# A hybrid encoder step on one core: the MLP's up projection in seven half-size products, its weight sums made by DMAs, and the last stage laid out anew

## What is computed

```python
p = einsum('btd,de->bte', rmsnorm(x, norm_mix), w_in)      # 10 column groups
...                                                        # heads A (stick-breaking), B (chunk band), C (HGRN2)
h = x + einsum('bte,ed->btd', mixed, w_o)                  # w_o: 1024 x 1024
u = relu(einsum('btd,df->btf', rmsnorm(h, norm_ffn), w_up))  # w_up: 1024 x 4096
y = h + einsum('btf,fd->btd', u * u, w_down)               # w_down: 4096 x 1024
```

## Time and profile before

| | us |
|---|---|
| executions | 3015.17, 3015.88, 3016.10 |
| median | 3015.88 |
| span of the profiled execution | 3009.8 |
| TensorE busy / VectorE busy / ScalarE busy / GpSimd busy | 2917.5 / 1630.4 / 987.6 / 327.6 |
| last stage, from its first transpose to the end | 1688.2 |

### The profile page before, as it was taken

One profiled execution on the slowest core, in us unless ns is written; L12 is line 12 of the kernel. 1 busy time (PEld: TensorE's weight loads), 2 busy tenths in 40 slices (PEclk: granted clock), 3 DMA queues, 4 the chain that ended last, 5 costly groups with the idle time before them and its releaser, 6 DMA issues.

```text
span 3009.8 us, 45644 instructions
## 1 busy us (share of the span) xinstructions
PE 2917.5 (97%) x18136; PEld 2585.7 (86%) x18136; DVE 1630.4 (54%) x2259; ACT 987.6 (33%) x1826; POOL 327.6 (11%) x504
## 2 busy tenths in 40 slices
PE   7999899899999999879999999999999999999999
PEld 5788788788888999768999999889999997888887
DVE  5554354476566577844444544544445445455555
ACT  3331266455555333233222222222222222232221
POOL 2322200020001255620000000000000000000000
PEclk9999999999999999989999999999999999999999
DMA  7833332453223553513211211332111213333332
GB/s 257 257 130 123 107 90 71 126 159 112 73 86 91 174 153 111 184 68 112 70 57 57 82 59 71 133 104 72 56 57 59 82 70 110 118 126 126 126 133 98
DMA packets 285061, 327.29 MB, mean 109 GB/s; under 512 B 53644, under 2 KB 234478, under 8 KB 284850
## 3 DMA queue, kind: packets, MB, share of 16 engines
q1 hardware_dynamic: 284850, 324.38, 32.8%
HBM read 256.28 MB, written 67.78 MB: 108 GB/s over the span
## 4 chain that ended last, share of the span: by engine, by line
PE 54%; DVE 1%; ACT 0%; issue 0%; POOL 0%; POOLq 0%; ACTq 0%
PE mf_psO L2260 28%; PE mf_psT L2312 23%; PE mf_psO L2312 1%; PE mf_psO L2283 1%; PE mf_psT L2246 1%; PE mf_psO L2295 0%; ACT mf_whi L2040 0%; DVE mf_wlo L2119 0%; DVE mf_acc L2212 0%; DVE mf_acc L2222 0%; DVE mf_xlo L2131 0%; ACT mf_hs L2101 0%; DVE mf_acc L2141 0%; DVE mf_hs L2149 0%; ACT mf_xhi L2055 0%
## 5 line engine op out<-in xcount | busy, mean ns | idle before, releaser
L2212 DVE TENSOR_TENSOR mf_acc<-mf_psO,mf_acc 128x1024 f32<-128x1024 f32 x256 | 313.5, 1225 | 347.8 <-PE mf_psO L2260 346.7
L2312 PE MATMUL mf_psT<-mf_xhi,mf_wlo 128*128 128x384 f32 (+1 forms) x1440 | 459.7, 319 | 0.0
L2312 PE MATMUL mf_psT<-mf_xlo,mf_whi 128*128 128x384 f32 (+1 forms) x1440 | 459.6, 319 | 0.0
L2312 PE MATMUL mf_psT<-mf_xhi,mf_whi 128*128 128x384 f32 (+1 forms) x1440 | 459.4, 319 | 0.0
L2260 PE MATMUL mf_psO<-mf_whi,mf_uhi 128*128 128x512 f32 x1024 | 401.5, 392 | 4.0 <-DVE mf_acc L2212 2.2
L2260 PE MATMUL mf_psO<-mf_whi,mf_ulo 128*128 128x512 f32 x1024 | 399.3, 390 | 0.0
L2260 PE MATMUL mf_psO<-mf_wlo,mf_uhi 128*128 128x512 f32 x1024 | 399.2, 390 | 0.0
L2040 ACT ACTIVATE mf_whi<-mf_st 128x2048 fp32r<-128x2048 f32 x104 | 194.8, 1911 | 605.1 <-PE mf_psO L2260 603.2
L2312 PEld LDWEIGHTS mf_psT<-mf_xhi,mf_whi 128*128 128x128 f32 x1440 | 270.5, 188 | 1.6
L2312 PEld LDWEIGHTS mf_psT<-mf_xlo,mf_whi 128*128 128x128 f32 x1440 | 270.5, 188 | 1.6
L2312 PEld LDWEIGHTS mf_psT<-mf_xhi,mf_wlo 128*128 128x128 f32 x1440 | 270.5, 188 | 0.0
(11 more groups left out here) (209 smaller groups left out, 5536.8 us busy)
## 6 DMA issues: line engine op xcount, KB each, us to landing
mf_st<-in_w_up SPq DMA_DIRECT2D x48, 1024.0 KB, 6.4
mf_st<-in_w_down SPq DMA_DIRECT2D x48, 1024.0 KB, 4.9
wst<-in_w_in SPq DMA_DIRECT2D x24, 1024.0 KB, 5.3
pj_wst<-in_w_in SPq DMA_DIRECT2D x36, 512.0 KB, 6.1
scratch_proj<-pj_ob SPq DMA_DIRECT2D x48, 256.0 KB, 2.0
pj_xin<-in_x_prompt SPq DMA_DIRECT2D x16, 512.0 KB, 7.3
md_qn<-scratch_proj SPq DMA_DIRECT2D x64, 128.0 KB, 2.6
scratch_proj<-md_ob SPq DMA_DIRECT2D x64, 128.0 KB, 3.3
```

Of the source, the lines that this page charges most:

```text
L2212: nc.vector.tensor_tensor(acc[0:r, i, :], psO[k % 2][0:r, :], acc[0:r, i, :], ALU.add).then_inc(s["o_out"], 1)
L2312: last = nc.tensor.matmul(up_psum(t, f, b, cn), wa[b4][:, w0:w0 + P], xa[:, j, c0:c0 + cn], start=j == 0 and q == 0, stop=j == KD - 1 and ...
```

## The change

**The up projection.** w_up is taken as two by two blocks of 512 rows and 2048 columns (W11, W12 above, W21, W22 below), and a third's frames as even tiles and odd tiles. The product of two by two blocks is made of seven products of half-size blocks in place of eight, by a variant of Strassen's form. Step p now has the features p and p + 16. Its seven products are 1 (W11), 2 (W21), 4 (W22), 5 (W12 + W22), 6 (W11 + W12 + W22), 7 (W11 + W12) and 3 (the sum of all four), each 12 matmuls of 384 (272) columns (`up`, 4 blocks of 128 rows and three parts). The frames' side has seven factors too: four are the blocks, and three (`full_sum`, `hi_sum`, `lo_sum`; with `xh6` four slots per pair of tiles) are sums, made per pair of tiles as the output projection goes on.

**PSUM.** Products 6, 5 and 3 are added on top of product 1 in one bank. Before each of them ScalarE copies what stands there (`snap`), and TensorE waits for it. VectorE adds up the four results (`add`, four instructions), ScalarE does relu and the high part of the square, VectorE squares and subtracts (`lo_u`).

**The sums of w_up** are made in HBM (`scratch_sums`, 4 x 4 MB): GpSimd issues four copies at turn 8 of `plan`, two adding DMAs at a third of it, one at its half, one at two thirds. It waits for the copies ahead of the first addition, and for each addition ahead of the next.

**The last stage.** Weights of the up projection come in chunks of 256 KB (512 rows of 512 bytes) to four staging places, and are split in 512 columns into seven pairs `uw`; those of the down projection are split in four parts. The weights of w_o lie over `u` and `uw`, so two of their four pieces can be split only after all down projections of the third before. x is loaded to `acc`. Each tile's second transpose stands in the middle of the next tile's output projection. The last third begins with the new frames, and their w_down is read from the same staging place as the other tiles'.

```diff
+            def begin_sums():
+                for out, half in copied:
+                    nc.gpsimd.dma_start(out, half).then_inc(sum_begun, 16)
+
+            def add_halves():
+                pool.wait_ge(sum_begun, 64)
+                for out, half in added[0:2]:
+                    nc.gpsimd.dma_start(out, half, accum_op=ALU.add, max_dma_last_dim=8192).then_inc(sum_added, 16)
...
+            beside = {masks_at: make_masks, 8: begin_sums}
+            for k, do in enumerate((add_halves, add_third, add_fourth)):
+                beside[len(plan) * (2 + k) // 6] = do
+            run(Dn.gpsimd(pool), B.gpsimd(pool), A.gpsimd(pool), C.gpsimd(pool), beside)
+            pool.wait_ge(sum_added, 64)
...
+        LEADS = [(0, 1), (0, 2), (1, 1), (1, 2), (0, 6), (1, 6), (0, 7), (0, 5), (0, 4), (0, 3), (1, 7), (1, 5), (1, 4), (1, 3)]
+        UPS = (1, 2, 6, 7, 5, 4, 3)
...
+            def snap(t, p, z):
+
+                act.wait_ge(s["up_done"], up_no(t, p, {1: 1, 2: 6, 4: 5}[z]) + 1)
...
+                nc.scalar.activation(kept_at(t, p, z), bank(t, p, 1), ACT.Copy).then_inc(s["snap"], 1)
...
+            def add(t, p, c):
+
+                if c == 21:
+                    dve.wait_ge(s["snap"], s_no(t, p, 2) + 1)
+                    dve.wait_ge(s["up_done"], up_no(t, p, 7) + 1)
+                    nc.vector.tensor_tensor(v_at(t, p, c), bank(t, p, 7), v_at(t, p, c), ALU.add).then_inc(s["v_begun"], 1)
+                    dve.wait_ge(s["v_begun"], NP * t + p + 1)
+                    dve.wait_ge(s["up_done"], up_no(t, p, 4) + 1)
+                    nc.vector.tensor_tensor(v_at(t, p, c), v_at(t, p, c), bank(t, p, 4), ALU.subtract
+                                            ).then_inc(s["v_ready"], 1)
+                    return
...
+                if z in (6, 5, 3):
+                    pe.wait_ge(s["snap"], s_no(t, p, {6: 1, 5: 2, 3: 4}[z]) + 1)
+                out = bank(t, p, 1 if z in (6, 5, 3) else z)
+                again = z in (6, 5, 3)
+                b, (wh, wl) = FACTOR[z], uw[c % NRING]
+                for kk in range(KH):
+                    for q, (wa, xa) in enumerate(((wh, xhb(b)), (wh, xlb(b)), (wl, xhb(b)))):
+                        last = nc.tensor.matmul(out, wa[:, kk, :], xa[:, kk, 0:HB[t]],
+                                                start=not again and kk == 0 and q == 0,
+                                                stop=kk == KH - 1 and q == 2, skip_group_check=again)
+                last.then_inc(s["up_done"], 1)
...
-                for f, b in up_order[:2]:
-                    up(f, b)
-                turn(t, nt - 1, True)
...
+                for at, (p, z) in enumerate(LEADS):
+                    if at == 2:
+                        turn(t, NTS[t] - 1, True)
+                    up(t, p, z)
+                down(t, 0)
+                for p in range(2, NP):
+                    for z in UPS:
+                        up(t, p, z)
+                    down(t, p - 1)
+                down(t, NP - 1)
```

1214 lines of the change are left out of this document (768 added, 446 removed).

## The result

| | before | after |
|---|---|---|
| median of the runs | 3015.5 us | 3062.2 us |
| ratio to before, 95% interval | | 1.0149 (1.0129 to 1.0168) |
| profiled execution | 3015.9 | 3049.6 |
| its span | 3009.8 | 3047.8 |
| mean granted clock of TensorE | 0.991 | 0.977 |

The kernel became 1.5% slower, where I had forecast 2.2% faster. The last two lines say where: the last stage gained 67.6 us (forecast 77.7), and what lies ahead of it lost 105.6 (forecast 12). Where the other three lost their 12 to 15 us no trace shows.

The account below looks back on a forecast made before the run. TensorE, busy 97% of the span, was taken as the bound. Gains of 90.8 and 8.9 less losses of 4, 11, 2, 5 and 12 gave -65.7: 3009.8 to 2944.1, with 6.1 around it 2950 us; range 2938 to 2965 (60%).

Parts of the forecast that it names:

- Matmuls, -90.8: Last stage: 192 fewer up projection matmuls per third at an unchanged pace, a gain of 90.8 us.
- a change of spacing as a sign of error: Whole kernel: the prediction is wrong if the spacing of matmuls changes; up projection expected at 0.173 and 0.126 us.
- The hole ahead of the last third, -8.9: Start of the last third: TensorE's 5.9 us wait and 3.0 us of slower clock go, gaining 8.9 us.
- Steady steps of two thirds, 0: Last stage, first two thirds: copies start in time, so TensorE never stalls; VectorE at 71%; 0 us.
- Steady steps of the last third, +4: Last third: VectorE at 88%, 0.3 us lost per 21.5 us step; loss 4 us, between 0 and 25.
- The rival of 2987: Last third: VectorE at 88% in strict order slips behind each copy, 32 us plus some 5; 2987 us, chance 14%.
- Leads, +11: Lead of each third: VectorE's work and the last tile's chain exceed their cover; loss 2.5 + 2.5 + 6 = 11 us.
- Output projection and boundaries, +7: Last stage: second transposes with little cover lose 2 us, late loads at the boundaries of thirds 2.5 x 2 = 5.
- Sums, +12, with 45 as the upper end: Middle stage: the eight DMAs' issues (5 us) and slower loads beside them (7 us) lose 12 us, between 0 and 45.
- Doubling them in the 155 us: Middle stage: loads take twice as long while the sums run, 155 of 980 us, and at its start; some 7 us.
- slower than before: Middle stage: adding DMAs delay small loads past their 8 us lead, 80 us plus 20 for GpSimd; 3050 us, chance 5%.
- Its point of decision: Middle stage: the slower-than-before rival decides where landing times of loads triple, from 2.6 us past the 8 us lead.

Follow-up runs that it names:

- e10: e9 with the last stage's tiles from the up projection's operands on (xh, xl, dwh, dwl and what follows) 32 bytes later in SBUF; 2940.0 us.
- e13: e9 with u, the ring, ident and ow shifted by 32 bytes as well; 2934.0 us, ratio 0.9734.
- e1: The changed kernel without the sums' eight DMAs, its last stage loading halves of w_up in place of the sums; 2947.9 us.
- e7: The changed kernel with only the four copies, all adding DMAs left out; 2988.4 us.
- e4: The changed kernel with the sums' DMAs asked for in rows of 2 KB instead of 8 KB; 3029.3 us.
- e3: The changed kernel with the sums made in 128 DMAs of 256 KB, one about every six turns; 2985.1 us.
- e6: As e3, same places, but in 32 DMAs of 1 MB; 2969.9 us.
- e8: As e3, but with the 128 DMAs placed between turns 60 and 600; 2983.2 us.
- e9: As e6, but with the 32 DMAs placed between turns 282 and 820; 2954.2 us.
- e11: The kernel before with the last stage's staging and weight tiles beginning 32 bytes later; 3033.1 us, ratio 1.0063.
- e12: e10 with u, the ring uw, ident and ow also beginning 32 bytes later; 2952.0 us.

## Why the prediction was wrong, point by point

1. *Matmuls, -90.8.* The count and the up projection's pace are right: 4032 products, 0.174 and 0.126 us apart. "Down and output projections keep their count" is right too, but I carried their pace over without a thought: 3888 products of 512 columns at 0.0045 to 0.0057 us more each are 21 us. Moving 32 bytes gave 14 to 20 us of it back (e10, e13). I had named a change of spacing as a sign of error, yet gave it no term.

2. *The hole ahead of the last third, -8.9.* Right: the wait of 5.9 us is gone, and TensorE's longest wait at that place is now 2.1 us, at a clock of 1.00.

3. *Steady steps of two thirds, 0.* Right: TensorE is busy 796.95 us of 800, and no wait for a `snap` copy appears. VectorE stood at 64% (71 expected).

4. *Steady steps of the last third, +4.* About right: the waits from 2720 us to the end are 2.8 us. VectorE was at 76%, not 88 (212.7 us of the 280 from 2720 on). A step lasts 22.9 us there and not 21.5, since I had given the new frames' small matmuls no time and the others are slower, and VectorE's durations, 18.9 us a step, overlap by 1.6. The rival of 2987 rested on the 88% and falls with it.

5. *Leads, +11.* Right: 2.4, 3.0 and 6.7 us of waits by the third, 12 in all, against 2.5, 2.5 and 6.

6. *Output projection and boundaries, +7.* Too high: 2.5 us of waits in the first (1.0 of them there before), none at the boundaries. This gives 5 us back. Another 6 are small waits that the kernel before had in this stage besides the hole and that are gone. Together they hide half of the 21 us of part 1: that the last stage came within 10 us of the forecast is in part luck.

7. *Sums, +12, with 45 as the upper end.* This is the step that failed: 105.6 in the trace, and 114 by the medians of after and e1. Three of its parts did so.
   - The issues: I took 3 us each, and they are 0.5 to 1.0 (the trace has 2.76 us for the four copies). Too high, and of no weight.
   - "A load beside it takes about twice its 2.6 us." I took the engines' share over the stage (0.34) and concluded that the sums fit. They do, but an issue of 4 or 16 MB isn't spread over the stage. It runs at once at a share of 0.99 to 1.07, and in that time a load takes 17 to 29 us. My own figures had it: copies that take "52 us of all engines" are a burst of 52 us (59 measured), six times the lead of 8 or more.
   - "Doubling them in the 155 us" then gave 7 us. What counts in a burst isn't each load's delay times the number of loads, but for how long of the burst TensorE runs dry. Of the 49 us after the copies it was idle 29; the stage lost 92 us to holes and 14 to the lower clock behind them. The clock had no place in part 7, though part 2 had used it.

The rival "slower than before" (3050, against 3062 measured) had the mechanism nearly right and the chance wrong: 5%. Its point of decision, landing times that triple beyond the lead, was passed by far beside the copies. That its number came so near is luck: it went wrong in ways that cancelled. It blamed the adding form with its rows of 8 KB alone, but plain copies cost 41 us (e7), and smaller rows bring only a quarter or so back (24 of 105.6 us in the traces of e4 and after). It spread the loss over 40 steps of 2 us, where it was a handful of long waits, TensorE's three longest of 17 to 28 us. And it gave 20 us to GpSimd waiting in its queue for a sum: in the trace of after GpSimd has no such wait. I gave it 5% since "rows show no such load while the stage's own share is 0.34": an average was used against an event. That all DMAs share 16 engines I had quoted from the Trainium skill in the prediction, and the trace agrees with it; but I used it for the amount of traffic, 7 us, and not for the waiting.

## What to carry to other kernels

A large DMA in the background is priced by how long what goes out at once fills the engines, against the lead of the smallest loads and stores beside it, not by its share of a stage's traffic: where 16 MB were issued at once the stage lost 41 us, and the whole sums cost 6 when cut in 32 pieces of 1 MB and put behind the first attention block. Cutting alone doesn't spread: look in the trace when the pieces really go out, since an engine with nothing to wait for runs ahead of its place in the plan (27 pieces in 23 us in e3). The other end has a price too: each issue takes 0.5 to 0.9 us of GpSimd, so the pieces should be as large as the lead allows. And when tiles are laid out anew, look at the spacing of matmuls that weren't touched: 32 bytes of offset were worth 14 to 20 us here.

## What the runs showed of the hardware

- Beside copies of 4 x 4 MB from HBM to HBM a load of 128 KB landed in 26 to 29 us (3.3 before), one of 32 KB in 17 (1.8 before), and a store held its buffer for 31. The copies took 59 us together, the engines moving 331 GB/s in all; two additions of 4 MB took 45 us, with 221 GB/s in all, and one alone 24 to 26.
- With packets of 4 KB in place of 8 KB (rows of 2 KB asked for) the same loads landed in 16 to 18 and 9 us, and the copies took no longer.
- In the first attention block 7 to 17 MB that went out at once cost 2.1 to 2.5 us per MB, in pieces of 256 KB, 1 MB or 4 MB alike (e3, e6, e8, e7).
- Beside 128 issues of GpSimd in place of none, VectorE's 451 instructions of the stage's end took 243 us in place of 222 (e3); 32 issues made it 224 (e6).
- The end of the stage on GpSimd took 3.3 us with up to 32 of its DMAs in it and 10.8 us with 128.
- A matmul of 128 x 128 with 512 columns follows the last after 0.2330 to 0.2333 us where the two operands in SBUF lie 32 bytes apart against a step of 64 (down projection, e9, e11, e12). Where they lie alike it is 0.2272 (before, e13's first two thirds), 0.2289 (e10) or 0.2333 (every second tile of e13's last third); what tells these apart is open. With 384 columns no such difference shows.
